# Local attention: band probabilities normalised on ScalarE head by head, reciprocals first in a step, meta part turned once and used in full-row products

## The chip, the cores and the metric

One core of one Trainium2 chip runs the whole program in one launch. The metric is the device time in microseconds (us). TensorE (PE) does matrix products and transposes into PSUM, VectorE (DVE), ScalarE (ACT) and GpSimd (POOL) do the rest, and SyncE (SP) issues the loads of the weights. Each engine works through its own list of instructions in order; semaphores tie the lists together.

## The reference

The program is two networks one after the other. The change lies in the first one, in its mixing layer, and there in the attention over a window:

```python
# 512 real tokens in 4 blocks of 128, 16 meta tokens in front, 16 query heads, 4 key/value heads, head width 64
def block_fn(args):
    n, qn, kn, vn = args                                   # one block of 128 queries
    keys = jnp.concatenate([k_meta, kn], axis=1)           # 16 meta keys, then the block before and this block
    vals = jnp.concatenate([v_meta, vn], axis=1)
    sc = jnp.einsum('bqkgd,bskd->bkgqs', qn, keys)
    valid = band_ok & ((n - 1) * BLOCK + kj >= 0)
    mask = jnp.concatenate([meta_ok, valid], axis=1)
    p = sink_softmax(sc, mask, sink)                       # softmax over the keys and one sink per head
    return jnp.einsum('bkgqs,bskd->bqkgd', p, vals)
```

The result is gated (`sigmoid(g_attn) * attn`), added to the gated result of a state-space layer, and projected. The outputs of meta-token queries are dropped later, so the kernel computes the 512 real queries alone.

## The kernel before

The attention is cut into 16 items `i`, one for each key/value head `g = i // 4` and query block `n = i % 4`. An item has four query heads. Its keys are a meta part (16 keys, `ki = 0`), the block before (128 keys, absent for `n = 0`) and its own block (128 keys). The scores of an item are [128 queries, 4 heads, 272 keys], or 144 keys for `n = 0`.

The items run through a software pipeline of 20 steps, written out by hand in `window_pe`, `window_act` and `window_dve` (L2001 to L2080). In step `i`:

- TensorE does the value products of item i-4 (`values_pe`), the second part of a weight unit, the transposes of item i-3 (`turn_pe`), the scores of item i (`scores_pe`), and the first part of a new weight unit. The weight units are the projections for later heads (`q`, `ga`, `gs`), eight chunks of three fp32r products each, spread over the steps by `CHUNKS` and `END`. `begun(i)` and `ended(i)` say which units begin and end in a step; `soon(i)` is true where fewer than three chunks stand ahead of the transposes. It is true in steps 0 to 5, 9, 13, 15 and 17 to 19.
- VectorE does, in this order, the scaled and masked scores, their maximum and the small operations on it for item i-1 (`softmax_dve`), the gating of the products of item i-4 (`values_dve`), the scaling of a finished projection (`q_ga_dve`), the normalising of item i-2 (`normalise_dve`), the low part of the next weight unit (`feed_lo`, L567) and the copy of one transposed part of item i-3 (`turn_copy`), the last two in the other order where `soon(i)`; then one piece of the side work for the state-space layer (`y_dve`).
- ScalarE does the copies of the transposed parts of item i-3 first where `soon(i)`, then the exponentials of item i-1 (`softmax_act`, four of them with the sum kept, one per head), the high part of the next weight unit (`feed_hi`, L552), the copies if not `soon(i)`, and a tanh.

Buffers: scores are held three deep (`S4`), the meta part of the normalised probabilities goes to a padded tile `S0`, 32 columns per head of which 16 are used. The transposed probabilities have one tile, `PT`. In PSUM, banks 4 to 7 hold scores, bank 3 holds the weight unit, and banks 0 to 2 go round among value products and transposes (`bk.limit(3)`, `bk.take`): an item with three key parts takes four of them in a step (product, three transposes), so the third transpose (L1918, `ki = 2`) takes the bank of the same step's product of item i-4 and waits until `values_dve` has read it.

The meta values are kept in a tile `VB`, [64, 4, 128], zero but for two blocks of 16 rows; two transposes of 64 columns and one product with both head pairs go with it. `VB` and the three `S0` tiles are set to zero on GpSimd in `window_pool` when the state-space layer is over, the VectorE fills in the values (L2050), and only then scales the first projection (L870), whose bank TensorE takes next.

Of the kernel before, what the change touches and what calls it, by code (L numbers as in the profile page):

```python
# [9 lines left out]
ACT = mybir.ActivationFunctionType  # L10
# [258 lines left out]
def program(nc, A, out):  # L269
    with ExitStack() as ctx:  # L270
# [115 lines left out]
        VB = mB("VB", [64, 4, 128])  # L386
# [1501 lines left out]
        def normalise_dve(e, i):  # L1888
            S_, z = S4[i % 3], sst[:, i % 4, :, :]
            ntot = 272 if i % 4 else 144  # L1890
# [3 lines left out]
            e.reciprocal(z[:, 6, :], z[:, 5, :]).then_inc(*s_dv.up())  # L1894
# [4 lines left out]
            for dst, o0, o1 in ((s0[:, :, 0:16], 0, 16), (S_[:, :, 16:ntot], 16, ntot)):  # L1899
                e.tensor_tensor(dst, S_[:, :, o0:o1], z[:, 6, :].unsqueeze(2).to_broadcast([128, 4, o1 - o0]),  # L1900
                                MUL).then_inc(*s_dv.up(("n", i)))
# [4 lines left out]
        def turn_pe(e, i):  # L1906
            kpos = 0
            s_dv.wait_ge(e, ("n", i))
            for ki, (_, kn) in enumerate(spans(i % 4)):
                b = bk.take(e, ("tr", i, ki))  # L1910
                if ki == 0:
                    for rr in range(2):
                        t = e.transpose(psum[0:64, b, 128 * rr:128 * rr + 128], S0[i % 3][:, 64 * rr:64 * rr + 64],
                                        ident[:, :])
# [7 lines left out]
        def turn_copy(e, i, on_act):  # L1922

            for ki, (_, kn) in enumerate(spans(i % 4)):
# [5 lines left out]
                rows, heads = (128, 4) if ki else (64, 2)  # L1930
                src = P(("tr", i, ki), 128 * heads, slice(0, rows))
                dst = PT[0:rows, ki, 0:heads, :].rearrange("p r n -> p (r n)")
# [5 lines left out]
        def values_pe(e, i):  # L1938
# [6 lines left out]
            for ki in range(len(keys)):  # L1945
                (s_dv if ki % 2 else s_cp).wait_ge(e, ("pt", i, ki))
            e.matmul(psum[:, b, 0:256], VB[:, g, :], PT[0:64, 0, 0:2, :].rearrange("p r n -> p (r n)"), start=True,
                     stop=False)
            for ki, (k0, kn) in enumerate(keys[1:], 1):
                for odd in range(2):  # L1950
                    t = e.matmul(psum[64 * odd:64 * odd + 64, b, 0:256], V[:, (k0 - 16) // 128 + 1, 64 * g:64 * g + 64],  # L1951
                                 PT[:, ki, 2 * odd:2 * odd + 2, :].rearrange("p r n -> p (r n)"), start=False,
                                 stop=ki == len(keys) - 1)
# [30 lines left out]
        def window_pool(e):  # L1984
# [8 lines left out]
            for t in [VB[:, :, :]] + [s[:, :] for s in S0]:  # L1993
                e.memset(t, 0.0).then_inc(*s_pool.up("VB0"))
# [23 lines left out]
        def window_act(e):  # L2018
# [9 lines left out]
            for i in range(20):  # L2028
                if 3 <= i <= 18 and soon(i):
                    turn_copy(e, i - 3, True)  # L2030
                if 1 <= i <= 16:
# [1645 lines left out]
```

## Time and profile before

| | |
|---|---|
| three runs | 2638.35, 2639.12 (median), 2644.05 us |
| the profiled execution | 2639.17 us, of which the span in the profile is 2637.4 us |
| granted TensorE clock over the span | 0.996 of full speed |
| busy share over the span | PE 98%, DVE 63%, ACT 40%, POOL 13% |
| the steps of the attention pipeline | about 550.5 to 699 us of the span |
| busy in 552 to 700 (148 us) | PE 143.62, DVE 120.97, ACT 67.86, POOL 8.34 us |

A row of the timeline gives start, duration, engine, line, operation, output and inputs; in brackets the idle time of that engine just before it and what ended it. A row can hold several equal instructions (x4): its duration then goes from the start of the first to the end of the last. Neighbouring instructions of one engine overlap by about 0.1 us (0.15 us and more on TensorE), so what an instruction occupies is best read from start to start. Lines L579 to L581 are the three products of a chunk, L567 and L552 the low and the high parts of a weight unit; other lines stand for themselves.

### The profile page before, as it was taken

Reading aid. Unit: us, or ns where it says so; the run is one execution under the profiler, and the core shown is the slowest. Engines: PE = TensorE matmul, PEld = TensorE weight load, DVE = VectorE, ACT = ScalarE, POOL = GpSimd, SP = SyncE. Lnnn points to the kernel's source line nnn. Section 1 sums busy time; section 2 is a strip of 40 time slices with the busy share of each in tenths; the row PEclk is TensorE's granted clock in tenths of the full one; section 3 lists DMA queues with packets and bytes.
Section 4 is the critical chain, followed back from the end, with each engine's and each line's share of the span. In section 5 each row is a group of like instructions: output and inputs, shape, how many; then the busy total and the mean of one; then the engine's idle time right before and its main releaser. Section 6 shows DMA issues by size and latency. Waiting matters only on the chain.

```text
span 2637.4 us, 35323 instructions
## 1 busy us (share of the span) xinstructions
PE 2582.7 (98%) x14596; PEld 2220.1 (84%) x14596; DVE 1673.8 (63%) x2605; ACT 1042.4 (40%) x1682; POOL 344.5 (13%) x361
## 2 busy tenths in 40 slices
PE   7999999999999999999999999999999999999999
PEld 7999999976688888887788788888898879888887
DVE  6854755758656534536774777647765477765765
ACT  4222233234434322235562545424454355433435
POOL 1133423020001000011000050000222014000031
PEclk9999999899999999999999999999999999999999
DMA  5243344431133233322121222332332222233332
GB/s 151 91 130 107 104 141 123 165 95 37 44 117 100 81 111 105 92 80 68 38 75 57 69 88 88 96 99 83 110 104 84 77 81 74 79 120 96 92 93 64
DMA packets 292823, 244.39 MB, mean 93 GB/s; under 512 B 19885, under 2 KB 285623, under 8 KB 292663
## 3 DMA queue, kind: packets, MB, share of 16 engines
q1 hardware_dynamic: 282599, 226.49, 27.5%
q0 software_dynamic: 5616, 13.48, 1.7%
q8 instruction: 115, 1.88, 0.3%
q10 hardware_dynamic: 4448, 2.16, 0.3%
q14 instruction: 45, 0.37, 0.0%
HBM read 230.80 MB, written 13.40 MB: 93 GB/s over the span
## 4 chain that ended last, share of the span: by engine, by line
PE 84%; DVE 9%; ACT 4%; issue 2%; DMA 1%; POOL 1%; SPq 0%; ACTq 0%; POOLq 0%; DVEq 0%
PE ps L579 26%; PE ps L580 26%; PE ps L581 26%; DVE ul L567 2%; ACT uh L552 1%; PE ps L2536 1%; PE ps L785 1%; PE ps L2508 1%; PE ps L1607 1%; PE ps L1853 0%; PE ps L1951 0%; DVE rbuf L800 0%; DVE tmp L2927 0%; DVE HL L2930 0%; PE ps L1918 0%
## 5 line engine op out<-in xcount | busy, mean ns | idle before, releaser
L567 DVE TENSOR_TENSOR ul<-raw,uh 128x1024 fp32r<-128x1024 f32 (+3 forms) x416 | 525.3, 1287 | 333.4 <-ACT uh L552 332.7
L579 PE MATMUL ps<-OH,uh 128*128 128x512 f32 (+1 forms) x1736 | 645.5, 372 | 4.5 <-DVE ul L567 3.8
L581 PE MATMUL ps<-OH,ul 128*128 128x512 f32 (+1 forms) x1736 | 638.6, 368 | 0.0
L580 PE MATMUL ps<-OL,uh 128*128 128x512 f32 (+1 forms) x1736 | 638.4, 368 | 0.0
L552 ACT CAST uh<-raw 128x1024 fp32r<-128x1024 f32 (+3 forms) x416 | 412.4, 1025 | 163.4 <-PE ps L581 116.0
L579 PEld LDWEIGHTS ps<-OH,uh 128*128 128x128 f32 x1736 | 327.3, 189 | 65.6 <-DVE ul L567 5.7
L580 PEld LDWEIGHTS ps<-OL,uh 128*128 128x128 f32 x1736 | 327.4, 189 | 54.7 <-issue 1.9
L581 PEld LDWEIGHTS ps<-OH,ul 128*128 128x128 f32 x1736 | 327.3, 189 | 54.6
L579 PE MATMUL ps<-HH,uh 128*128 128x512 f32 (+2 forms) x946 | 319.4, 338 | 0.6 <-DVE HL L2930 0.2
L580 PE MATMUL ps<-HL,uh 128*128 128x512 f32 (+2 forms) x946 | 317.3, 335 | 0.0
L581 PE MATMUL ps<-HH,ul 128*128 128x512 f32 (+2 forms) x946 | 317.3, 335 | 0.0
L579 PE MATMUL ps<-XH,uh 128*128 128x264 f32 (+1 forms) x992 | 310.5, 313 | 5.7 <-DVE tmp L1144 2.9
L580 PE MATMUL ps<-XL,uh 128*128 128x264 f32 (+1 forms) x992 | 304.9, 307 | 0.0
L581 PE MATMUL ps<-XH,ul 128*128 128x264 f32 (+1 forms) x992 | 304.3, 307 | 0.0
L579 PEld LDWEIGHTS ps<-XH,uh 128*128 128x128 f32 x992 | 188.0, 189 | 25.0 <-issue 16.2
L579 PEld LDWEIGHTS ps<-HH,uh 128*128 128x128 f32 x946 | 178.2, 188 | 21.3 <-DVE HL L2930 2.3
L581 PEld LDWEIGHTS ps<-XH,ul 128*128 128x128 f32 x992 | 188.3, 190 | 8.5
L580 PEld LDWEIGHTS ps<-XL,uh 128*128 128x128 f32 x992 | 188.1, 190 | 7.1
L580 PEld LDWEIGHTS ps<-HL,uh 128*128 128x128 f32 x946 | 178.2, 188 | 18.3 <-issue 0.5
L581 PEld LDWEIGHTS ps<-HH,ul 128*128 128x128 f32 x946 | 178.3, 188 | 18.2
L816 POOL TENSOR_TENSOR acc<-acc,tmp 128x512 f32<-128x512 f32 (+2 forms) x56 | 69.4, 1239 | 668.9 <-ACT tmp L806 664.6
L2701 POOL TENSOR_TENSOR acc<-H 128x512 f32<-128x512 f32 x4 | 8.6, 2151 | 939.7 <-DVE H L2940 621.1
(457 smaller groups left out, 3704.7 us busy)
## 6 DMA issues: line engine op xcount, KB each, us to landing
raw<-in_ffn_w SPq DMA_DIRECT2D x40, 1024.0 KB, 5.2
raw<-in_ffn_w_up SPq DMA_DIRECT2D x40, 1024.0 KB, 5.0
raw<-in_ffn_w SPq DMA_DIRECT2D x32, 704.0 KB, 4.3
raw<-in_ffn_w_down SPq DMA_DIRECT2D x32, 704.0 KB, 4.4
raw<-in_w_in SPq DMA_DIRECT2D x16, 1024.0 KB, 5.7
raw<-in_gla_w_in SPq DMA_DIRECT2D x12, 1024.0 KB, 5.2
raw<-in_mla_w_o SPq DMA_DIRECT2D x8, 1024.0 KB, 4.8
raw<-in_ple_w_gate SPq DMA_DIRECT2D x8, 1024.0 KB, 5.2
```

The source lines that it names most:

```text
L552: e.copy(h, src).then_inc(*s_whi.up((u, j)))
L567: e.tensor_tensor(l, src, h.bitcast(F32), SUB).then_inc(*s_wlo.up(("unit", u)))
L579: e.matmul(o, wh, xh, start=first, stop=False)
L580: e.matmul(o, wh, xl, start=False, stop=False)
L581: return e.matmul(o, wl, xh, start=False, stop=last)
L785: i = e.matmul(psum[:, b, 0:n], ones[:, :], tile[:, t0:t0 + n], start=j == 0, stop=j == len(parts) - 1)
L816: e.tensor_tensor(a, a, tmps[k - 1][:, t0:t0 + n], ADD).then_inc(*s_pool.up(*((tag, "acc", k, hf) for hf in hfs)))
L1607: t = e.matmul(psum[o0:o0 + n, b, 66 * g:66 * g + 66], mm[:, 0, 128 * g + c0:128 * g + c0 + n], UB[q][:, e0 + g, :], start=True, stop=True)
L2508: t = e.transpose(psum[:, b, o:o + 128], SS[h % 2][:, SO[n] + 128 * k:SO[n] + 128 * k + 128], ident[:, :])
L2536: t = e.matmul(psum[:, b, 128 * k:512], VT[:, k, 128 * (h % 2):128 * (h % 2) + 128], PTm[:, PO[k]:PO[k] + 512 - 128 * k], start=k == 0, st ...
L2701: e.tensor_tensor(a, HV[:, 0, :], HV[:, 1, :], ADD).then_inc(*s_pool.up((xt, "two")))
```

## The change

On VectorE, `normalise_dve` moves from behind `values_dve` and the projection's scaling to the start of the step, and keeps of the multiplications only the one of the meta part into `S0`. The multiplication of the band part (128 or 256 columns per head) becomes four activations on ScalarE with the reciprocal as a per-partition scale (`normalise_act`), ahead of the exponentials of the next item. The transposes wait for both. The meta part is transposed with one full transpose of [128, 128] in place of two of 64 columns; the copy to `PT` is [128, 128] in place of [64, 256]. The meta value products are two, each over all 128 rows and 128 columns, with two tiles `VB[0]`, `VB[1]` of [128, 4, 128] (the second lies in `tmps[1]`), and they come behind the band products in the accumulation, so that the wait for the ScalarE copy of the meta part stands behind the band products. GpSimd zeroes two such tiles, and VectorE fills in four blocks.

```diff
--- before.py
+++ after.py
@@ -383,7 +383,7 @@
         mk0 = mB("mk0", [128, 272])
         sst = mB("sst", [128, 4, 8, 4])
         snk = mB("snk", [128, 16])
-        VB = mB("VB", [64, 4, 128])
+        VB = [mB("VB0", [128, 4, 128])[:, :, :], tmps[1][:, 0:512].rearrange("p (g n) -> p g n", g=4)]
         S0 = [mB(f"S0{i}", [128, 128]) for i in range(3)]
         mC = Sbuf(nc, rest)
         ML = mC("ML", [128, 8, 512], F32R)
@@ -1887,18 +1887,26 @@
 
         def normalise_dve(e, i):
             S_, z = S4[i % 3], sst[:, i % 4, :, :]
-            ntot = 272 if i % 4 else 144
             s_fn.wait_ge(e, ("e", i))
             e.tensor_tensor(z[:, 5, :], z[:, 3, :], z[:, 4, :], ADD).then_inc(*s_dv.up())
             s_dv.wait_ge(e, NOW)
-            e.reciprocal(z[:, 6, :], z[:, 5, :]).then_inc(*s_dv.up())
+            e.reciprocal(z[:, 6, :], z[:, 5, :]).then_inc(*s_dv.up(("rz", i)))
             s_dv.wait_ge(e, NOW)
             s0 = S0[i % 3][:, :].rearrange("p (r n) -> p r n", r=4)
             if i == 0:
                 s_pool.wait_ge(e, "VB0")
-            for dst, o0, o1 in ((s0[:, :, 0:16], 0, 16), (S_[:, :, 16:ntot], 16, ntot)):
-                e.tensor_tensor(dst, S_[:, :, o0:o1], z[:, 6, :].unsqueeze(2).to_broadcast([128, 4, o1 - o0]),
-                                MUL).then_inc(*s_dv.up(("n", i)))
+            if i > 2:
+                s_mm.wait_ge(e, ("tr", i - 3))
+            e.tensor_tensor(s0[:, :, 0:16], S_[:, :, 0:16], z[:, 6, :].unsqueeze(2).to_broadcast([128, 4, 16]),
+                            MUL).then_inc(*s_dv.up(("n", i)))
+
+        def normalise_act(e, i):
+            S_, z = S4[i % 3], sst[:, i % 4, :, :]
+            ntot = 272 if i % 4 else 144
+            s_dv.wait_ge(e, ("rz", i))
+            for r in range(4):
+                e.activation(S_[:, r, 16:ntot], S_[:, r, 16:ntot], ACT.Identity, scale=z[:, 6, r:r + 1]).then_inc(
+                    *s_fn.up(("n", i)))
 
 
 
@@ -1906,12 +1914,11 @@
         def turn_pe(e, i):
             kpos = 0
             s_dv.wait_ge(e, ("n", i))
+            s_fn.wait_ge(e, ("n", i))
             for ki, (_, kn) in enumerate(spans(i % 4)):
                 b = bk.take(e, ("tr", i, ki))
                 if ki == 0:
-                    for rr in range(2):
-                        t = e.transpose(psum[0:64, b, 128 * rr:128 * rr + 128], S0[i % 3][:, 64 * rr:64 * rr + 64],
-                                        ident[:, :])
+                    t = e.transpose(psum[:, b, 0:128], S0[i % 3][:, :], ident[:, :])
                 else:
                     for r in range(4):
                         o = 128 * (2 * (r % 2) + r // 2)
@@ -1927,9 +1934,9 @@
                 if i:
                     s_mm.wait_ge(e, ("pv", i - 1))
                 s_mm.wait_ge(e, ("tr", i, ki))
-                rows, heads = (128, 4) if ki else (64, 2)
-                src = P(("tr", i, ki), 128 * heads, slice(0, rows))
-                dst = PT[0:rows, ki, 0:heads, :].rearrange("p r n -> p (r n)")
+                heads = 4 if ki else 1
+                src = P(("tr", i, ki), 128 * heads)
+                dst = PT[:, ki, 0:heads, :].rearrange("p r n -> p (r n)")
                 if on_act:
                     e.copy(dst, src).then_inc(*bk.free(s_cp, ("tr", i, ki), ("pt", i, ki)))
                 else:
@@ -1942,15 +1949,14 @@
             for v in range(5):
                 (s_cp if v % 2 else s_dv).wait_ge(e, ("V", v))
             s_dv.wait_ge(e, "VB")
-            for ki in range(len(keys)):
+            for ki, (k0, kn) in enumerate(keys[1:], 1):
                 (s_dv if ki % 2 else s_cp).wait_ge(e, ("pt", i, ki))
-            e.matmul(psum[:, b, 0:256], VB[:, g, :], PT[0:64, 0, 0:2, :].rearrange("p r n -> p (r n)"), start=True,
-                     stop=False)
-            for ki, (k0, kn) in enumerate(keys[1:], 1):
                 for odd in range(2):
-                    t = e.matmul(psum[64 * odd:64 * odd + 64, b, 0:256], V[:, (k0 - 16) // 128 + 1, 64 * g:64 * g + 64],
-                                 PT[:, ki, 2 * odd:2 * odd + 2, :].rearrange("p r n -> p (r n)"), start=False,
-                                 stop=ki == len(keys) - 1)
+                    e.matmul(psum[64 * odd:64 * odd + 64, b, 0:256], V[:, (k0 - 16) // 128 + 1, 64 * g:64 * g + 64],
+                             PT[:, ki, 2 * odd:2 * odd + 2, :].rearrange("p r n -> p (r n)"), start=ki == 1, stop=False)
+            s_cp.wait_ge(e, ("pt", i, 0))
+            for rr in range(2):
+                t = e.matmul(psum[:, b, 128 * rr:128 * rr + 128], VB[rr][:, g, :], PT[:, 0, 0, :], start=False, stop=rr == 1)
             t.then_inc(*s_mm.up(("pv", i)))
 
         def values_dve(e, i):
@@ -1990,7 +1996,7 @@
             s_pool.wait_ge(e, "m1")
             e.affine_select(out=mk0[:, 144:272], in_=mk0[:, 144:272], compare_op=ALU.is_ge, fill=NEG, base=0,
                             pattern=[[-1, 128]], channel_multiplier=1).then_inc(*s_pool.up("mask"))
-            for t in [VB[:, :, :]] + [s[:, :] for s in S0]:
+            for t in VB + [s[:, :] for s in S0]:
                 e.memset(t, 0.0).then_inc(*s_pool.up("VB0"))
             sk = A["attn_sinks"]
             e.dma_start(snk[:, :], bass.AP(tensor=sk.tensor, offset=sk.offset, ap=[[0, 128], [1, 16]])).then_inc(
@@ -2028,6 +2034,8 @@
             for i in range(20):
                 if 3 <= i <= 18 and soon(i):
                     turn_copy(e, i - 3, True)
+                if 2 <= i <= 17:
+                    normalise_act(e, i - 2)
                 if 1 <= i <= 16:
                     softmax_act(e, i - 1)
                 for name, c in begun(i):
@@ -2046,15 +2054,18 @@
             e.tensor_copy(KS[64:128, :, :], K[0:64, :, :]).then_inc(*s_dv.up("KS"))
             s_pool.wait_ge(e, "VB0")
             s_dv.wait_ge(e, ("V", 0))
-            for p0, o0 in ((0, 0), (32, 64)):
-                e.tensor_copy(VB[p0:p0 + 16, :, o0:o0 + 64], V[0:16, 0, :].rearrange("p (g n) -> p g n", g=4)).then_inc(
-                    *s_dv.up("VB"))
+            for r in range(4):
+                o0 = 64 * (r % 2)
+                e.tensor_copy(VB[r // 2][32 * r:32 * r + 16, :, o0:o0 + 64],
+                              V[0:16, 0, :].rearrange("p (g n) -> p g n", g=4)).then_inc(*s_dv.up("VB"))
             for name, c in HEAD:
                 if c or name != "q":
                     feed_lo(e, name)
                 q_ga_dve(e, name, c)
             side = Steps()
             for i in range(20):
+                if 2 <= i <= 17:
+                    normalise_dve(e, i - 2)
                 if 1 <= i <= 16:
                     softmax_dve(e, i - 1)
                 if i >= 4:
@@ -2064,8 +2075,6 @@
                         scale_dve(e, ("gs", 0, 0), tmps[0][:, 0:512], rmix, ("gs in", 0))
                     else:
                         q_ga_dve(e, name, c)
-                if 2 <= i <= 17:
-                    normalise_dve(e, i - 2)
                 if not soon(i):
                     for name, c in begun(i):
                         feed_lo(e, name)
```

## Rows read from the trace of the kernel before

**Rows 1.** The page's part 4: the chain that ended last, by engine.
```profile
PE 84%; DVE 9%; ACT 4%; issue 2%; DMA 1%; POOL 1%; SPq 0%; ACTq 0%; POOLq 0%; DVEq 0%
```

**Rows 2.** Busy time by stretch: stretch, length, busy us (count) of each engine, clock, DMA.
```profile
552.00:700.00 148.00, 143.62 (x808) 102.00 (x807) 120.97 (x245) 67.86 (x204) 8.34 (x16) 1.00 0.16 47
```

**Rows 3.** Waits in 552 to 700: who for whom, us in total, times, longest.
```profile
ACT S L1883 <- DVE sst L1875: 34.8, 11, 6.2
DVE ul L567 <- ACT uh L552: 12.8, 12, 1.8
...
PE ps L1947 <- DVE PT L1936: 2.4, 3, 1.1
...
PE ps L1947 <- ACT PT L1934: 1.1, 3, 0.6
PE ps L1918 <- DVE Mg L1963: 0.8, 1, 0.8
```

**Rows 4.** Timeline of VectorE, steps 5 and 6.
```profile
589.83 0.48 DVE L1963 SCALAR_TENSOR_TENSOR Mg<-Mg,ps 128x128 f32<-128x128 f32 x2
...
590.83 0.15 DVE L1892 TENSOR_TENSOR sst<-sst 128x4 f32<-128x4 f32 x1
...
591.23 1.36 DVE L1900 TENSOR_TENSOR S<-S,sst 128x64 f32<-128x64 f32 x2
...
594.57 1.23 DVE L567 TENSOR_TENSOR ul<-raw,uh 128x1024 fp32r<-128x1024 f32 x1 [1.38 <-ACT uh L552]
...
596.80 1.28 DVE L1866 SCALAR_TENSOR_TENSOR S<-ps,mk 128x1088 f32<-128x1088 f32 x1
...
599.79 0.47 DVE L1963 SCALAR_TENSOR_TENSOR Mg<-Mg,ps 128x128 f32<-128x128 f32 x2
```

**Rows 5.** Timeline of ScalarE, steps 4 and 5.
```profile
582.41 0.52 ACT L1883 ACTIVATE S<-S,sst 128x272 f32<-128x272 f32 x1
...
584.54 1.04 ACT L552 CAST uh<-raw 128x1024 fp32r<-128x1024 f32 x1
...
591.32 0.59 ACT L1934 COPY PT<-ps 128x512 f32<-128x512 f32 x1 [0.45 <-PE ps L1918]
591.80 0.42 ACT L1883 ACTIVATE S<-S,sst 128x144 f32<-128x144 f32 x1
...
593.50 1.04 ACT L552 CAST uh<-raw 128x1024 fp32r<-128x1024 f32 x1
594.44 0.63 ACT L1977 ACTIVATE Mg<-Mg 128x512 f32<-128x512 f32 x1
```

**Rows 6.** Timeline of TensorE: starts of the transposes of steps 4, 5, 6; step 16.
```profile
580.64 0.38 PE L1913 MATMUL ps<-ident,S 128*64 128x128 f32 x2
...
590.02 0.38 PE L1913 MATMUL ps<-ident,S 128*64 128x128 f32 x2
590.24 1.04 PE L1918 MATMUL ps<-ident,S 128*128 128x128 f32 x8
...
599.85 0.38 PE L1913 MATMUL ps<-ident,S 128*64 128x128 f32 x2
...
683.76 0.66 PE L1918 MATMUL ps<-ident,S 128*128 128x128 f32 x4 [0.78 <-DVE Mg L1963]
```

**Rows 7.** Timeline of GpSimd at the head of the stage.
```profile
536.78 0.52 POOL L1994 MEMSET VB<- 64x512 f32 x1
```

**Rows 8.** Timeline of VectorE at the head of the stage.
```profile
537.76 0.59 DVE L2050 COPY VB<-V 16x256 f32<-16x256 f32 x2 [1.51 <-POOL S L1994]
538.39 1.29 DVE L870 TENSOR_TENSOR Q<-ps,mbuf 128x512 f32<-128x512 f32 x2
```

**Rows 9.** Timeline of TensorE at the head of the stage.
```profile
539.23 0.47 PE L579 MATMUL ps<-XH,uh 128*128 128x512 f32 x1 [1.42 <-DVE Q L870]
```

**Rows 10.** Groups by line and shape, whole span: busy us, mean ns of one, idle before.
```profile
L2816 ACT ACTIVATE OH<-H,cv 128x256 fp32r<-128x256 f32 x64 | 32.1, 508 | 43.9 <-DVE H L2779 43.7
...
L1900 DVE TENSOR_TENSOR S<-S,sst 128x1024 f32<-128x1024 f32 x12 | 14.6, 1217 | 0.0
```

## The prediction

> **What bounds the kernel now.** I read the chain that ended last first: 84% of it is TensorE [rows 1], so any wait that TensorE is given is paid in full, and work taken off another engine is worth only the waits that it ends. Next the busy time of the stretch with the 20 steps: of 148 us TensorE is busy 143.6, VectorE 121, ScalarE 68 [rows 2]. Then who waits for whom there. TensorE's waits come to 2.4 + 1.1 + 0.8 = 4.3 us in seven places [rows 3]. ScalarE waits 34.8 us in 11 of the steps for VectorE's maximum; in the other five nothing is listed, and VectorE itself waits 12.8 us for the high part of the weight unit that ScalarE makes behind its exponentials. So the two feed each other in a ring that runs through all steps. A timeline of the three engines over steps 4 to 6 says how tight it is.
>
> **The ring.** Where `soon(i)`, ScalarE begins a step with the copies. Follow step 5 into step 6. TensorE's third transposes start at 590.24 + 4 x 0.11 = 590.68 [rows 6]; the copy of them starts at 591.32, the exponentials at 591.80, the high part at 593.50 [rows 5], the low part at 594.57, and after it and a piece of side work (2.23 together) the scores' operations at 596.80, the gating at 599.79, done at 600.26 [rows 4]. Only then may TensorE's next third transposes start, since they take the bank just read. They were due at 599.85 + 0.22 + 0.44 = 600.51 [rows 6]. The ring takes 9.58 us, some 0.1 more with the signal; TensorE needs 9.83. The margin is about 0.15 us. From step 4 to 5 it is the same: third transposes at 581.30, exponentials at 582.41 for 2.13 us [rows 5], gating done at 590.31 [rows 4], next ones due at 590.68: margin 0.3. In step 16 the margin is gone already, and TensorE waits 0.78 us for the gating [rows 6].
>
> **The change, part by part.**
>
> *The band part leaves VectorE.* It takes 1.22 us of an item with 272 keys [rows 10]. In the old order it stood behind the gating, where VectorE ended up waiting 1.38 us for the high part anyway [rows 4]. In the steps in which it waits so, the saving is worth nothing. It is worth something in the steps where TensorE waits for the VectorE copy behind it (2.4 us in all, rows 3).
>
> *Reciprocals first.* The two small operations take 591.23 - 590.83 = 0.40 us, the meta part 1.36 - 1.22 = 0.14 [rows 4]. These 0.55 us now stand between the low part and the scores' operations, on the ring, in every step. Queued behind them are the maximum, for which ScalarE waits, and the gating, for which TensorE's bank waits.
>
> *Four activations on ScalarE.* The nearest row is an Identity activation of 256 columns with a per-partition operand: 508 ns, of which consecutive ones overlap about 0.1 [rows 10], so 0.41 each, 1.64 an item; about 0.3 each, 1.2 an item, for 128 columns. From below, a cast of 1024 columns occupies 593.50 to 594.44 [rows 5], a quarter of it is 0.235, 0.94 an item. From above, an exponential of 272 columns with its sum read out occupies 2.13 / 4 = 0.53 less the read, some 0.42. I take 0.41. In the eleven steps where ScalarE waits for VectorE they hide in that wait. Where the step begins with the copies, ScalarE is held by TensorE, the maximum is ready when the copies are done, and the 1.64 us go onto the ring in front of the exponentials; the high part, the low part and the next step's scores are queued behind them.
>
> The Trainium skill, page "ScalarE: Activation LUTs", section "What ACT_TABLE_LOAD costs", gives 280 ns + 0.833 ns a column for a pointer operand, with 93 ns overlap back to back: 0.40 by its figures as an estimate, and the row's 508 ns agrees. By its formula for immediate operands it would be 0.31, which is not this form. The same page's rules for kernel authors say to keep a multiplication on VectorE, and the sum below agrees.
>
> *So step 5 to step 6* takes 9.68 + 1.64 + 0.55 = 11.87 us by the ring, while TensorE has 9.83 less 0.27 (next paragraph) = 9.56: a new wait of 2.3 us. Step 4 to 5: 9.0 + 0.1 + 2.19 = 11.3 against 9.38 - 0.27 = 9.1: 2.2 us.
>
> *Transposes and products.* One transpose less an item at 0.11 [rows 6]: 1.8 us less over 16 items. The meta products keep their columns (2 x 128 for 1 x 256) but load twice as many weights, full 128 x 128; their place behind the band products may hide one start, which I count as 0.16 an item. From the other side, if a load is laid bare, +0.1 to +0.2 an item. The copy of the meta part gets about 0.1 shorter. Where TensorE waits for the ring, none of this moves the end.
>
> *The head.* TensorE waits 1.42 us there for VectorE's first scaling [rows 9], that stands behind two fills (0.63 us for two, start to start), and these behind GpSimd's zeroing [rows 8]. The change adds a second tile (0.52 long, about 0.46 start to start [rows 7]) and two fills (0.62): +1.1 us on TensorE, nothing covers it.
>
> **The sum.** I carried the same arithmetic through all steps, with the occupied times of these rows and the waits that the code has (copies before products, gating before third transposes, a scaled projection before bank 3 is taken again). For the order of before it gives 4.8 us of waits on TensorE against 4.3 in the trace, at the same places. For the new order it gives: at third transposes, step 4 1.9, step 5 2.1, step 6 2.3, step 9 0.6, step 10 2.3, step 14 2.3, step 16 2.2, step 18 0.4; at products, step 7 0.3, step 8 1.45, step 9 0.25, step 11 0.3, step 12 1.4, step 13 0.95, step 15 0.3, step 17 0.4. That is 19.5, so 14.7 more; less 16 x 0.27 = 4.3; plus 1.1 at the head: +11.5 us. With 0.235 for an activation it is +7.3. Between the two, and near the first, I take +10.5. Behind step 19 TensorE runs without a gap into the next products, so the whole difference stays. The profiled execution took 2639.17 us, its span 2637.4; the median of the runs is 2639.12, the same. Forecast: 2639.1 + 10.5 = 2649.6 us, the bounds of the activation's and the products' costs giving 2646 to 2652.5.
>
> **Rivals.**
> 1. *VectorE was the bound and is relieved: faster.* For it: VectorE is 82% busy in these steps, ScalarE 46% [rows 2], and TensorE's 4.3 us of waits are nearly all for copies behind the old place of the normalising [rows 3]. If the 0.55 us and the 1.64 us find slack that I don't see, these go, and with them 1.8 us of transposes, against 1.1 at the head: -5.0, with the 0.16 an item of the products -7.6; say -6, 2633 us. Against: the margin of 0.15 us read above. It decides if the activations cost under about 0.2 us each and the reciprocals don't delay the maximum. Chance 0.10. The Trainium skill, "Perfetto Trace Analysis", section "Optimizing Scalar/DVE Operations", says that with VectorE saturated moving operations to ScalarE may make sense; that is this case, and by it the time would be this one.
> 2. *The activations hide, the rest doesn't.* If ScalarE had room in the steps with copies too, only the 0.55 us on the ring and the head would be left. The same sum with activations at nothing gives +2.5 and the head 1.1: +3.6, 2642.7 us. For it: ScalarE's 34.8 us of waiting. Against: none of that lies behind a copy in these steps, rows 5 show the exponentials 0.48 us behind the copy. Chance 0.12.
> 3. *Weights laid bare as well.* Four full loads an item not hidden (+0.2) and the ring as forecast: one or two us more, 2651.5; it is inside the range. Chance 0.08.
> 4. *The forecast*, 0.70.
>
> **The numbers.** A change of less than 0.2% (5.3 us) can hardly be told from none here. Slower by more than that: forecast and rival 3, 0.78. Within it: rival 2, 0.12. Faster by more: rival 1, 0.10 (its upper half would count as no change; I leave it there). The range of 8 in 10 goes down to rival 2 and a little below, 2641, and up to 2653.5.
>
> **What would show it.** In the profile after: TensorE waits for L1963 at the third transposes in steps 4, 5, 6, 10, 14 and 16, 2 us each, against one of 0.8 now; TensorE's idle time before the first product behind the head about 2.5 us for 1.42; four activations between the copies and the exponentials in steps 4, 5, 9, 13, 15, about 0.41 us from start to start; VectorE's busy time down 17 us without gain, its wait for the high part up. It is wrong if the maximum of an item comes no later than before, or if the activations occupy 0.2 us.

## The result and the profile after

The changed kernel takes 2659.52 us (median of 5 runs, 2653.38 to 2663.26), the kernel before on the same chip 2641.87 (5 runs, 2638.35 to 2644.05): a ratio of 1.0065 [1.0054, 1.0076], 17.65 us slower. The forecast was 2649.6 and its range ended at 2653.5. Of the 9.9 us between forecast and result 2.8 are the kernel before itself, which was put at 2639.1. The sign and the reason given were right, as the rest shows, and the size was too small: there is a second loss, that of TensorE's clock, that the forecast had no term for.

The page of the changed kernel: span, engines, and the chain that ended last by engine.

```profile
span 2657.7 us, 35402 instructions
PE 2593.0 (98%) x14612; PEld 2231.0 (84%) x14612; DVE 1658.6 (62%) x2591; ACT 1064.8 (40%) x1746; POOL 345.6 (13%) x362
PE 82%; DVE 10%; ACT 5%; issue 2%; DMA 1%; POOL 1%; SPq 0%; ACTq 0%; POOLq 0%; DVEq 0%
```

TensorE is on the chain for 82% [rows 1 had 84%]; what it lost went to VectorE and ScalarE, which now release it more often. Its waits in the stage that was changed are the first thing to see. TensorE's timeline of the changed kernel (start, length, instruction, idle time before it and its releaser), the long waits:

```profile
543.50 0.76 PE L579 MATMUL ps<-XH,uh 128*128 128x512 f32 x1 [2.55 <-DVE Q L870]
...
588.38 0.66 PE L1925 MATMUL ps<-ident,S 128*128 128x128 f32 x4 [1.77 <-DVE Mg L1969]
...
599.64 0.66 PE L1925 MATMUL ps<-ident,S 128*128 128x128 f32 x4 [1.92 <-DVE Mg L1969]
...
611.48 0.66 PE L1925 MATMUL ps<-ident,S 128*128 128x128 f32 x4 [0.52 <-DVE Mg L1969]
...
625.68 0.65 PE L1955 MATMUL ps<-PT,V 128*64 128x256 f32 x4 [1.25 <-DVE PT L1943]
...
636.49 0.66 PE L1925 MATMUL ps<-ident,S 128*128 128x128 f32 x4 [0.77 <-DVE Mg L1969]
...
648.40 0.86 PE L1925 MATMUL ps<-ident,S 128*128 128x128 f32 x4 [2.18 <-DVE Mg L1969]
...
686.45 0.66 PE L1925 MATMUL ps<-ident,S 128*128 128x128 f32 x4 [2.08 <-DVE Mg L1969]
...
700.74 0.66 PE L1925 MATMUL ps<-ident,S 128*128 128x128 f32 x4 [2.06 <-DVE Mg L1969]
```

The first is the head, 2.55 us where [rows 9] had 1.42. The others are third transposes of steps 4, 5, 6, 9, 10, 14 and 16 and one product of step 8. One such wait of 0.78 us stood in the trace of before [rows 6]. In all, 13.05 us in ten places in this stage against 4.28 in seven [rows 3].

The second loss is seen in the clock. Busy time by stretch of the changed kernel (stretch, length, busy us and count of PE, PEld, which is TensorE loading weights, DVE, ACT, POOL, granted clock, DMA share, GB/s): the head, the stage from the first scores to the last product, and two stretches of 10 us behind the waits of steps 5 and 10.

```profile
535.10:556.10 21.00, 18.45 (x77) 14.39 (x75) 5.15 (x9) 4.42 (x5) 12.01 (x26) 0.92 0.23 45
556.10:712.70 156.60, 143.41 (x815) 104.95 (x814) 104.25 (x226) 89.13 (x265) 8.37 (x16) 0.97 0.15 45
600.00:610.00 10.00, 10.00 (x46) 6.97 (x45) 5.47 (x10) 6.63 (x20) 0.00 (x0) 0.83 0.02 8
650.00:660.00 10.00, 10.00 (x44) 7.17 (x43) 6.72 (x14) 6.97 (x21) 0.00 (x0) 0.72 0.00 0
```

The same two stretches of the kernel before:

```profile
532.00:550.50 18.50, 17.08 (x74) 13.35 (x73) 4.57 (x7) 4.42 (x5) 11.50 (x25) 1.00 0.31 68
550.50:696.40 145.90, 141.52 (x802) 101.05 (x801) 119.97 (x242) 66.63 (x201) 8.34 (x16) 1.00 0.16 48
```

Before, the granted clock is 1.00 in both. After, it is 0.92 and 0.97, and TensorE is busy in every microsecond of 600 to 610 at 0.83 and of 650 to 660 at 0.72: it works, at the lower of its two levels (1.2 for 2.4 GHz) for part of the time. TensorE's timeline behind the wait of step 5 shows it product by product:

```profile
601.71 0.79 PE L579 MATMUL ps<-XH,uh 128*128 128x512 f32 x1
...
602.30 0.63 PE L580 MATMUL ps<-XL,uh 128*128 128x512 f32 x1
602.73 0.63 PE L581 MATMUL ps<-XH,ul 128*128 128x512 f32 x1
```

From one start to the next it is 0.43 us for the 0.23 of the same product elsewhere. It stays so for about 3.4 us, in which 1.7 us of full-speed work is not done. Below, such a stretch at the lower level is called a fall. The fall behind step 10 is twice as long, 3.4 us lost; the one at 542 in the head begins within the wait and costs about 1.3.

The clock differs ahead of the changed code too. The two kernels from 400 us to the head, before and changed:

```profile
400.00:532.00 132.00, 130.87 (x1040) 124.30 (x1039) 86.72 (x181) 38.91 (x63) 25.33 (x48) 0.95 0.48 154
400.00:535.15 135.15, 134.10 (x1042) 127.12 (x1040) 86.63 (x181) 38.86 (x63) 25.55 (x48) 0.92 0.49 153
```

The ledger, from the profiled executions (2659.52 and 2639.17 us, 20.35 apart):

| stretch | before | after | difference | of it |
|---|---|---|---|---|
| up to the head | 532.00 | 535.15 | +3.15 | ahead of the changed code; the head begins between 530.4 and 535.2 in the twelve profiles. Read in slices of 2 us, the clock lost 10.2 us there for 6.8 before: 3.4 more |
| head | 18.53 | 20.92 | +2.4 | wait +1.1, a fall +1.3 |
| stage | 145.85 | 156.67 | +10.8 | idle +8.8, two falls +5.1, less work -3.2 |
| rest | 1941.0 | 1945.0 | +4.0 | a fall at 726 +1.7, behind a wait of 2.12 us that the kernel before has too; 2.3 not placed |

The row of the stage adds up what stands there; it doesn't say what the stage would take without the falls. e8 below answers that, and the answer is not 5.1 us less.

### The profile page after: what moved, and what is told of

Read it like the earlier page. It is cut to its first block, busy times and chain, and to the rows that moved or that the text cites. A ratio compares the mean times of both kernels' runs of the same rounds, so it can differ in the third digit from the quotient of the medians.

```text
span 2657.7 us, 35402 instructions
## 1 busy us (share of the span) xinstructions
PE 2593.0 (98%) x14612; PEld 2231.0 (84%) x14612; DVE 1658.6 (62%) x2591; ACT 1064.8 (40%) x1746; POOL 345.6 (13%) x362
## 4 chain that ended last, share of the span: by engine, by line
PE 82%; DVE 10%; ACT 5%; issue 2%; DMA 1%; POOL 1%; SPq 0%; ACTq 0%; POOLq 0%; DVEq 0%
PE ps L579 25%; PE ps L581 25%; PE ps L580 25%; DVE ul L567 2%; ACT uh L552 1%; PE ps L2545 1%; PE ps L785 1%; PE ps L2517 1%; ACT S L1883 1%; PE ps L1607 0%; DVE rbuf L800 0%; ACT S L1908 0%; DVE S L1866 0%; DVE sst L1870 0%; PE ps L1853 0%
```

## The experiments

All times stand beside runs of the kernel before on the same chip: 2641.55 us (31 runs) for e1 to e4, 2642.10 (16) for a0 and e5 to e7, 2640.14 (12) for e8 and e9. "Stage" is the stretch of the profile from the first scores to the start of the last item's value products, 145.85 us before; "clock" the mean granted clock over the span, a mean over the runs. The kernel before had 0.9952, 0.9950 and 0.9959 on the three chips.

| kernel | us (runs) | ratio | stage | clock |
|---|---|---|---|---|
| e1 head alone | 2644.07 (10) | 1.0003 [0.9994, 1.0012] | 145.86 | 0.9944 |
| e2 transposes and products alone | 2641.94 (10) | 1.0001 [0.9991, 1.0011] | 143.58 | 0.9942 |
| e3 reciprocals first alone | 2644.64 (10) | 1.0015 [1.0005, 1.0025] | 149.63 | 0.9948 |
| e4 changed, activations last | 2646.70 (10) | 1.0016 [1.0006, 1.0025] | 146.69 | 0.9941 |
| a0 changed, again | 2658.66 (4) | 1.0065 [1.0048, 1.0082] | 159.86 | 0.9915 |
| e5 changed, head freed | 2653.59 (5) | 1.0043 [1.0028, 1.0058] | 159.65 | 0.9924 |
| e6 e5, activations last, reciprocals in their old place | 2635.70 (10) | 0.998 [0.997, 0.999] | 141.33 | 0.9949 |
| e7 changed, five waits filled | 2653.59 (6) | 1.0042 [1.0029, 1.0055] | 156.91 | 0.9947 |
| e8 changed, six waits filled | 2652.09 (6) | 1.0047 [1.0029, 1.0064] | 155.25 | 0.9950 |
| e9 changed, activations behind the high part | 2649.47 (7) | 1.0034 [1.0023, 1.0045] | 151.97 | 0.9941 |

**e1, the head alone.** The kernel before, with the second tile zeroed and filled.

```diff
-            for t in [VB[:, :, :]] + [s[:, :] for s in S0]:
+            for t in [VB[:, :, :], tmps[1][:, 0:512].rearrange("p (g n) -> p g n", g=4)] + [s[:, :] for s in S0]:
                 e.memset(t, 0.0).then_inc(*s_pool.up("VB0"))
...
+            for p0, o0 in ((64, 0), (96, 64)):
+                e.tensor_copy(tmps[1][:, 0:512].rearrange("p (g n) -> p g n", g=4)[p0:p0 + 16, :, o0:o0 + 64],
+                              V[0:16, 0, :].rearrange("p (g n) -> p g n", g=4)).then_inc(*s_dv.up("VB"))
```

> The kernel before with only the extra work at the head of the stage: a second tile zeroed on GpSimd and two more fills on VectorE ahead of the first scaling. Theory A (the head's wait is on the path, and a longer wait also costs TensorE's clock): TensorE's wait before the first product behind it goes from 1.42 to about 2.5 us, +1.1 us, and if the clock falls there as in the changed kernel (granted 0.83 in 540 to 550 us) another 1.2 us: +1 to +2.5 us against before. Theory B (the changed kernel's loss beyond the forecast comes from the products or from elsewhere): +1.1 at most and the clock stays at 1.00.

TensorE's timeline and two stretches of e1:

```profile
541.67 0.76 PE L579 MATMUL ps<-XH,uh 128*128 128x512 f32 x1 [2.54 <-DVE Q L870]
...
714.41 0.50 PE L579 MATMUL ps<-YH,uh 128*128 128x512 f32 x1 [2.12 <-DVE ul L567]
...
716.49 0.63 PE L580 MATMUL ps<-YL,uh 128*128 128x512 f32 x1
```
```profile
533.30:554.50 21.20, 18.66 (x74) 14.55 (x73) 5.15 (x9) 4.42 (x5) 12.00 (x26) 0.92 0.21 40
554.50:700.40 145.90, 141.47 (x802) 101.04 (x801) 120.02 (x242) 66.62 (x201) 8.36 (x16) 1.00 0.17 48
```

The wait is 2.54 us, 1.12 more: the term of the sum to a hundredth. But the head is 2.7 us longer, since the clock fell behind that wait. The first product is 0.76 us long there, for 0.47 in [rows 9]. The stage is the same as before. In the time of the run this is +2.5 us, which the interval of the ratio (0.9994 to 1.0012) doesn't tell from nothing. The second line is a lesson of its own: the wait of 2.12 us at 714 is also in the kernel before, where no fall followed; here one did.

```profile
710.42 0.50 PE L579 MATMUL ps<-YH,uh 128*128 128x512 f32 x1 [2.12 <-DVE ul L567]
```

So the same wait is followed by a fall in some executions and not in others.

**e2, the turned meta part and its products alone.** The changed kernel with the band multiplication back on VectorE and the whole normalising back in its old place.

```diff
+            e.tensor_tensor(S_[:, :, 16:ntot], S_[:, :, 16:ntot],
+                            z[:, 6, :].unsqueeze(2).to_broadcast([128, 4, ntot - 16]), MUL).then_inc(*s_dv.up(("n", i)))
...
-                if 2 <= i <= 17:
-                    normalise_act(e, i - 2)
```

> The changed kernel with all normalising back on VectorE at its old place in the step: what is left is the single transpose of the meta part, the full-row products behind the band products, and the head. Theory A (the ring through VectorE and ScalarE is the loss): the sum over the steps gives -2.4 us plus 1.1 at the head, -1.3 us against before, within -4 to +1; no third transpose waits more than 1 us. Theory B (the four full weight loads of the products are laid bare, or their place is bad): a large part of the +17.6 us stays, +5 us or more, and a value product block takes longer than 1.64 us.

The stage of e2:

```profile
556.30:699.90 143.60, 138.29 (x815) 102.53 (x814) 119.95 (x242) 64.95 (x201) 8.37 (x16) 1.00 0.17 49
```

It is 2.3 us shorter; the sum, carried through this order, says 2.4. TensorE's busy time falls from 141.52 to 138.29 us, 3.2, and its idle time rises by 0.9 where it now comes early; one third transpose waits 1.07 us, where none over 1 was expected. A block of products takes 1.05 us from start to start with two key parts (1.21 before) and 1.48 with three (1.64), a block of transposes 0.12 less: no full load of weights is laid bare. 16 x 0.27 = 4.3 would follow from the blocks, and 3.2 is what the stage shows. The run's time is that of before: in the profile the head is 3.2 us longer (21.71 for 18.53, a wait of 3.04 and a fall) and takes back what the stage gives.

**e3, the reciprocals first alone.** The kernel before; sum, reciprocal and meta part first in the step, the band part where it was.

```diff
             for i in range(20):
+                if 2 <= i <= 17:
+                    normalise_dve(e, i - 2)
...
                 if 2 <= i <= 17:
-                    normalise_dve(e, i - 2)
+                    band_dve(e, i - 2)
```

> The kernel before with the sum, the reciprocal and the meta part's multiplication first in VectorE's step, the band part's multiplication left on VectorE at the old place; ScalarE and TensorE as before. It puts 0.55 us on the ring and nothing else. Theory A: +4.5 us by the sum over the steps (4.5 us more of waits on TensorE, at third transposes), and up to 2 us more if the clock falls. Theory B (the order on VectorE is harmless, the activations are the whole loss): within 1 us of before.

The stage of e3:

```profile
550.80:700.50 149.70, 142.78 (x802) 101.00 (x801) 120.27 (x242) 66.49 (x201) 8.37 (x16) 1.00 0.16 47
```

+3.8 us by the stage, +3.8 by the mean of the runs, 4.5 by the sum. So 0.55 us of small operations ahead of the maximum, in each of 16 steps, cost 3.8 us in all, with the clock at 1.00. It is the ring without anything on ScalarE. TensorE's idle time accounts for 2.5 us of it (6.9 for 4.4); its busy time is 1.3 us longer with the same products, which I can't place.

**e4, the activations last.** The changed kernel, its four activations moved behind ScalarE's last copy of the step.

```diff
-                if 2 <= i <= 17:
-                    normalise_act(e, i - 2)
                 if 1 <= i <= 16:
...
                     turn_copy(e, i - 3, True)
+                if 2 <= i <= 17:
+                    normalise_act(e, i - 2)
```

> The changed kernel with the four activations of an item moved from the start of ScalarE's step to its end, behind the exponentials, the high part and the copies. Theory A: the 1.64 us leave the ring, the 0.55 us and the head stay: +2.5 us against before by the sum, 9 us less than the changed kernel's by the same sum, and more if its clock losses go too (up to 15 us faster than the changed kernel). Theory B (ScalarE's activations cost by contention or by ScalarE's busy time, wherever they stand): within 3 us of the changed kernel.

The stage of e4:

```profile
555.10:701.80 146.70, 138.78 (x815) 102.02 (x814) 104.38 (x226) 88.65 (x265) 8.33 (x16) 1.00 0.16 48
```

The same work on the same engines as in the changed kernel (compare ScalarE's 88.65 and 89.13 us), and the stage is 10.0 us shorter; the run's loss against the kernel before is 12 us smaller. Falls have a part in that: against e8, where the clock is 1.00 in the stage as here and the activations stand in front (155.25), it is 8.6 us. What costs is where the 1.64 us stand in ScalarE's order, not that ScalarE does them. The profiled execution of e4 had 5.78 us of waiting in its head, beginning 4.3 us earlier than that of the changed kernel; its stage alone is compared here. The stage is +0.8 over the kernel before, for 1.4 by the sum; the run is +4.9 by the means, for 2.5.

**a0 and e5, the head again.** a0 is the changed kernel. e5 puts the fills of the meta values inside the head's loop, behind the second scaling, so that TensorE doesn't wait for them.

```diff
                 q_ga_dve(e, name, c)
+                if (name, c) == ("q", 1):
+                    s_pool.wait_ge(e, "VB0")
+                    s_dv.wait_ge(e, ("V", 0))
+                    for r in range(4):
...
```

> The changed kernel as it is, again, beside the others. Theory A (ring waits, the head, and TensorE's clock falling after some of the long waits): +13 to +20 us against before, and a profile in which the stage from the first scores to the last product takes 152 to 158 us (145.85 before) with the clock under 1.00 in places that differ from the first profile. Theory B (the 6 us beyond the forecast were chance of the five first runs): +9 to +12 us.

> The changed kernel with the four fills moved behind the first two scalings, so that neither GpSimd's zeroing nor the fills stand ahead of the bank that TensorE waits for. Theory A: TensorE's wait there (2.55 us, before 1.42) goes, the clock stays at 1.00 in that stretch, the head falls from 20.9 to about 17.2 us: 2.5 to 4 us faster than the changed kernel. Theory B (the head is hidden by later waits of the ring): within 1 us of the changed kernel.

The head and the stage of e5, and its wait in step 6:

```profile
534.20:551.10 16.90, 16.90 (x77) 13.47 (x75) 5.24 (x9) 4.42 (x5) 12.05 (x26) 1.00 0.25 49
551.10:710.70 159.60, 144.87 (x815) 106.21 (x814) 104.47 (x226) 89.11 (x265) 8.33 (x16) 0.96 0.15 44
```
```profile
606.51 0.66 PE L1925 MATMUL ps<-ident,S 128*128 128x128 f32 x4 [2.10 <-DVE Mg L1969]
```

a0's time is inside the 13 to 20 us expected, its stage of 159.86 longer than the 152 to 158. In e5 TensorE is busy through the whole head at a clock of 1.00, which takes 16.9 us for the 21.15 of a0; the run is 5.1 us shorter than a0's (5.4 by the means, with 3.4 either way on these few runs; 2.5 to 4 expected). That no wait at all is left in the head is in part the state of this execution: VectorE and GpSimd are released there by a transfer (at 537.58 us), and e6, with the same head code, began its head 3.9 us earlier, was released at 536.32 and waited 1.93 us. Its stage is as long as a0's, with falls in other places (3.4 us lost behind the wait at 606, 3.4 at 682; a0 has 1.7, 3.4 and 3.4). In step 6 it waits 2.10 us, near the 2.3 of the forecast, where the profile after had 0.52: there TensorE came 1.7 us late itself, out of the fall behind step 5. A fall hides part of the next wait, so the two losses don't simply add.

**e6, the change in the order that the ring allows.** e5, with the activations last as in e4 and the reciprocals back where they were.

```diff
             for i in range(20):
-                if 2 <= i <= 17:
-                    normalise_dve(e, i - 2)
                 if 1 <= i <= 16:
...
+                if 2 <= i <= 17:
+                    normalise_dve(e, i - 2)
                 if not soon(i):
```

> A version meant to beat both: the changed kernel with the small operations and the meta part back at VectorE's old place, the four activations at the end of ScalarE's step, and the fills behind the first scalings; transposes and products as changed. Theory A: nothing is added to the ring, the band part's multiplication has left VectorE; the sum over the steps gives -3.7 us and the head -1.4: -5 us against before, 2636.5. Theory B (activations on ScalarE cost wherever they stand, or the products do): not faster than before.

The stage of e6, and its longest wait:

```profile
549.40:690.70 141.30, 138.03 (x815) 102.02 (x814) 104.42 (x226) 88.79 (x265) 8.34 (x16) 1.00 0.17 49
```
```profile
679.03 0.66 PE L1925 MATMUL ps<-ident,S 128*128 128x128 f32 x4 [1.35 <-DVE Mg L1969]
```

2635.70 us, faster than both: 6.4 under the kernel before (5.4 by the means; the ratio's interval ends at 0.999), 23 under the changed one. All three parts of the change are in it; only the order differs. The stage is 4.5 us shorter than before (3.7 by the sum): 3.5 of TensorE's work and 1.1 of its waits. Against e4 it is 5.4 us shorter, the price of the reciprocals first, which e3 gave as 3.8 in the other surroundings. And against e2 it is 2.3 us shorter (141.33 for 143.58, both at a clock of 1.00): with the reciprocals at their old place in both, that is what the move of the band part to ScalarE is worth where nothing queues behind it. The gain is in the stage; the head of this profile, 19.0 us, is no shorter than before (18.5), where 1.4 less was expected.

**e7 and e8, the clock alone.** The changed kernel, with products whose result nobody reads in front of the third transposes, where TensorE would wait. The order of everything else is kept. The products have 384 columns, where the expectation says 256, and a group takes 1.8 to 2.2 us: they fill the whole wait and not 1.2 us of it. They write a bank of the scores and wait until it is free, which takes 0.3 us in one step.

```diff
+        WARM = {1: 9, 2: 10, 7: 11, 11: 10, 13: 10}
...
+                if ki == 2 and i in WARM:
+                    if e is not COUNTING:
+                        s_dv.wait_ge(e, ("bank", ("sc", i + 2, 0)))
+                    for _ in range(WARM[i]):
+                        e.matmul(psum[:, 4, 0:384], MIX[0][:, 0, 16:144], MIX[0][:, 0, 16:400], start=True, stop=True)
```

e8 adds `3: 11`, the wait that e7 leaves.

> The changed kernel with 9 to 11 idle products of 256 columns (their result is never read) ahead of the third transposes of items 1, 2, 7, 11 and 13, where TensorE waits 1.8 to 2.2 us. They fill about 1.2 us of each wait and change nothing that another engine does. Theory A (the clock falls because TensorE stands still, and this costs time beyond the waits): the granted clock stays at 1.00 in the stage, where it lost 5.1 us' worth in the changed kernel, and the time is 1 to 5 us less than the changed kernel's. Theory B (the ring sets the pace and the clock only changes what is waiting): the clock may stay up, the time is within 1 us of the changed kernel's. If the clock falls as often as before, standing still was not what made it fall.

> As the run with idle products in five waits, with 11 more ahead of the third transposes of item 3 (step 6), where that run's profile still had a wait of 2.11 us and the clock fell behind it. Theory A (the clock falls only behind waits of about 2 us, and the forecast's sum holds where it does not fall): no fall between the first scores and the last product, that stage takes 10 to 12 us more than before (156 to 158 us) with the clock at 1.00 all through, and the time is 1 to 3 us under the run with five waits filled, about 2651. Theory B (the clock falls as often whatever stands in the waits): falls elsewhere in the stage and the same time as with five, 2653.6.

The stretch of e7 behind the wait that is left (2.11 us at 608):

```profile
610.00:620.00 10.00, 10.00 (x45) 7.23 (x44) 6.76 (x13) 6.43 (x21) 4.18 (x8) 0.72 0.47 132
```

The stage of e8, and the fill of step 6 with the third transposes behind it:

```profile
553.90:709.20 155.30, 150.19 (x878) 112.43 (x877) 104.20 (x226) 88.92 (x265) 8.36 (x16) 1.00 0.15 45
```
```profile
607.27 2.18 PE L1925 MATMUL ps<-XH 128*128 128x384 f32 x11
609.45 0.66 PE L1932 MATMUL ps<-ident,S 128*128 128x128 f32 x4
```

In e7 the clock falls in the stage only behind the one wait that is not filled; in e8 nowhere in it (its head still has a fall, with a wait of 2.54 us). TensorE works longer there, 150.19 us for 143.41, and the stage is shorter than that of the changed kernel (155.25 for 156.67; 159.86 in a0). The run of e7 is 5.1 us shorter than a0's beside it, 5.5 by the means (3.0 either way). e8 ran on another chip, so it is read against the kernel before: +12.0 us by the medians, +12.7 by the means, where e7 has +11.5 and +11.0. The 1 to 3 us under e7 that were expected of the sixth fill don't show in the runs; e8's mean clock is 0.0009 under that of the kernel before on its chip, e7's 0.0003.

The stage of e8 is what the ring costs with the clock kept: 155.25 - 145.85 = +9.4 us, for 14.7 - 4.3 = +10.4 by the sum (156 to 158 us were expected). Counting the fills as waits (150.19 less the 138.03 us that the same work takes in e6), TensorE waits 17.3 us in it for 4.4 before: +12.9 for the sum's 14.7, and its own work is 3.5 less for 4.3. The falls then add only what is left of them: the changed kernel's stage with 5.1 us of falls is 1.4 us longer than e8's, a0's with 8.5 us is 4.6 longer, e5's with 6.8 is 4.4 longer. The rest of the falls runs in time that TensorE would have waited.

**e9, the activations between.** The changed kernel, the activations behind the high part and ahead of the late copies.

```diff
                     feed_hi(e, name)
+                if 2 <= i <= 17:
+                    normalise_act(e, i - 2)
                 if 3 <= i <= 18 and not soon(i):
```

> The changed kernel with the four activations between the high part of the weight unit and the copies of ScalarE's step: off the ring through exponentials and high part in every step, but ahead of the copies where these come last. The forecast's sum gives +6.8 us against before (waits of 2 us at the products of items 5, 9, 13 for the ScalarE copies in place of those at third transposes). Theory A: +6 to +9 us, between the version with activations last (+4.2 measured) and the changed kernel (+16.6). Theory B (only the start of the step matters): as with activations last, within 1.5 us.

TensorE's waits in the stage of e9 (who for whom, us, times, longest):

```profile
PE ps L1955 <- ACT PT L1941: 5.8, 4, 2.1
PE ps L1925 <- DVE Mg L1969: 3.0, 6, 0.9
PE ps L1955 <- DVE PT L1943: 2.5, 2, 1.2
```

The waits move from the third transposes, 3.0 us now, to the products behind the late copy, 8.3. The stage is +6.1 over before, between e4 and the changed kernel, and the run +9.3 (+9.7 by the means), a little above the 6 to 9 expected. The waits of 11.3 us are nearly those of the changed kernel (13.05), but only one reaches 2 us, and the stage has lost little by the clock (0.99).

## Why the forecast was right in kind and short in size

**The ring was read rightly.** Long waits stand at the third transposes of steps 4, 5, 10, 14 and 16: 1.77, 1.92, 2.18, 2.08, 2.06 us for 1.9, 2.1, 2.3, 2.3, 2.2. Step 6 has 0.52, and 2.10 in e5, for 2.3. Steps 9 and 8: 0.77 and 1.25 for 0.6 and 1.45. The product waits forecast for steps 12 and 13 (1.4, 0.95) are 1.23 and 0.50 in e5. ScalarE's timeline of step 5, changed kernel, shows the new operations where they were put, behind the copy and ahead of the exponentials:

```profile
600.34 0.59 ACT L1941 COPY PT<-ps 128x512 f32<-128x512 f32 x1 [2.70 <-PE ps L1925]
600.82 1.70 ACT L1908 ACTIVATE S<-S,sst 128x256 f32<-128x256 f32 x4
602.42 0.40 ACT L1883 ACTIVATE S<-S,sst 128x144 f32<-128x144 f32 x1
...
604.12 1.03 ACT L552 CAST uh<-raw 128x1024 fp32r<-128x1024 f32 x1
```

From copy to exponentials it is 602.42 - 600.82 = 1.60 us more, 0.40 each for the 0.41 taken. From copy to high part it is 3.78 us; in [rows 5] 2.18. VectorE's timeline takes it from there:

```profile
605.18 1.23 DVE L567 TENSOR_TENSOR ul<-raw,uh 128x1024 fp32r<-128x1024 f32 x1 [4.39 <-ACT uh L552]
...
607.96 1.28 DVE L1866 SCALAR_TENSOR_TENSOR S<-ps,mk 128x1088 f32<-128x1088 f32 x1
...
610.95 0.48 DVE L1969 SCALAR_TENSOR_TENSOR Mg<-Mg,ps 128x128 f32<-128x128 f32 x2
```

It waits 4.39 us for the high part, [rows 4] 1.38, and the gating that frees TensorE's bank starts 611.0 - 600.3 = 10.6 us behind the copy, for 599.79 - 591.32 = 8.47: +2.1, the 1.64 + 0.55 of the forecast. The waits in the stage by engine:

```profile
DVE ul L567 <- ACT uh L552: 37.4, 13, 4.8
...
ACT S L1883 <- DVE sst L1875: 17.0, 10, 3.3
...
PE ps L1925 <- DVE Mg L1969: 11.8, 9, 2.2
```

VectorE's work fell by 15.7 us and its waiting for ScalarE rose by 24.6 [rows 3 had 12.8]. That is what became of "relieving" it, and why rival 1 fails; e6 shows that its gain is there in another order. Rival 2 fails as well: ScalarE's waiting was indeed halved (34.8 to 17.0 us), so the activations hide in part of the steps, as the forecast said, but the stage of e4 against that of e8, both with the clock at 1.00, shows 8.6 us for those that don't. Rival 3 fails by e2: the products got cheaper.

**The head** was right as a wait (1.13 and 1.12 more for 1.1).

**Transposes and products** were a little dear: the blocks gave 0.12 and 0.16 us an item as taken, but the stage's busy time 3.2 us for 4.3, by e2. I haven't found where the other 1.1 is.

**The step that failed is the sum itself: it has waits and work, and no term for the granted clock.** "That is 19.5, so 14.7 more; less 16 x 0.27 = 4.3; plus 1.1 at the head" prices a wait of TensorE at its length. The clock in [rows 2] was 1.00, and I took it to stay. Behind the new waits it did not. What is shown:
- The profile after has three falls that the kernel before has not (542, 600, 648), each with a wait of 1.9 to 2.6 us.
- Over all twelve profiles, between 530 and 760 us, 22 of the 40 waits of 1.7 us or more had a fall, begun in the wait or up to 1.3 us behind it, each of 1.7 or 3.4 us by the granted clock; of the 50 waits of 0.5 to 1.7 us none had. Of the waits of 1.7 us and more within the stage it was 9 of 19, and of the 11 that were filled none.
- Filling the waits, nothing else changed, keeps the clock in the stage (e8: 1.00) and makes the kernel faster (e7 against a0: 5.5 us by the means, 3.0 either way). It leaves +11.0 us in e7 and +12.7 in e8, where the sum gave +11.5.
- In the 59 runs of the kernel before the time is about 2 us lower for each 0.001 that the mean clock is higher. The changed kernel's is 0.0035 lower (0.9915 and 0.9950 in a0's comparison), an estimate of 7 of its 16.5 us. It goes by a relation between runs and shows no cause.

So of a0's 16.5 us some 5.5 to 7 are the clock and 9.5 to 11 the waits less the work saved. With the clock kept the stage is +9.4 us (e8) and the head's wait +1.1, together the 10.5 that the forecast took. That it agrees to the tenth is luck in part: 10.5 was a choice between two prices of an activation, and the sum had the waits too long (14.7 for about 12.9) and the saving too large (4.3 for 3.5), which offset each other.

**What stays open.** Why a wait of 2.1 us is followed by a fall in one execution and not in the next (710 before, 714 in e1) isn't settled. Nor are 2.3 us of the rest of the profile after. The 3.15 us ahead of the head are about the 3.4 us by which the clock lost more there; why it did isn't known. The count above holds for 530 to 760 us only: the kernel before has falls at 470 and 518 us too, where the waits listed in the ten microseconds before are 0.90 and 0.23 us, so 1.7 us is no limit for other code.

## What to carry to other kernels

Before work is moved to the engine with the lower busy share, follow one step around: if two engines feed each other in a fixed order, what counts is where in that order the operation stands. The same four activations take 8.6 us more of the stage ahead of the exponentials than behind the last copy (e8 and e4), and e6 turned the change from 17 us slower to about 6 us faster by order alone. And where TensorE bounds the kernel, price a new wait of about 2 us above its length: here about every second one came with a stretch at half speed, 1.7 or 3.4 us lost by the clock, part of which the next waits take up again. Waits of 0.5 to 1.7 us in these stretches had none.

## What the runs showed of the hardware

The fall of the clock comes behind single waits of about 2 us in a stage in which TensorE was 97% busy before (141.52 of 145.9 us); I had not thought that one such wait could do it. It came in 22 of 40 cases, no run shows what decides which, and between 530 and 760 us it lost 1.7 or 3.4 us each time, nothing between. Products that nobody reads, put into the wait, left no fall in any of the 11 places where they stood (five in e7, six in e8), and made the kernel faster (2658.66 to 2653.59 us for e7, run beside it): doing more work was quicker than waiting.
